# Interleaving the two groups of the SSD's B and C products on TensorE, over three pairs of banks

## The reference

```python
def ssd_chunked(x, a, bm, cm):
    ...
    scores = jnp.einsum('bclhn,bcshn->bhcls', cm, bm) * jnp.exp(segsum(a))
    y_diag = jnp.einsum('bclhs,bcshp->bclhp', scores, x)
    ...
def ssd_direction(xs, dt, a, bm, cm, reverse):
    heads_per_group = SSD_HEADS // SSD_GROUPS
    y = ssd_chunked(prep(xs * dt[..., None]), prep(dt * a),
                    prep(jnp.repeat(bm, heads_per_group, axis=2)),
                    prep(jnp.repeat(cm, heads_per_group, axis=2)))
```

## Time and profile before

| | |
|---|---|
| median of 3 runs | 2627.54 us (2627.06 to 2630.75) |
| span of the profiled execution, first to last instruction | 2628.6 us |
| TensorE busy | 2483.0 us, 94% |
| VectorE busy | 1365.9 us, 52% |
| ScalarE, GpSimd busy | 784.3 us, 1057.0 us |
| mean granted TensorE clock | 0.974 |
| CB stage, first load to end of last copy, layer 0 | 124.10 to 134.99 us |
| CB stage, layer 1 | 1431.64 to 1442.53 us |

### The profile page before, as it was taken

The page is one execution under the profiler, slowest core; times in us unless marked ns, Lnnn a source line. Parts: engine busy times, 40 slices in busy tenths (PEclk is TensorE's granted clock), DMA queues, the critical chain, the costliest instruction groups (busy, mean ns, idle before and its releaser), DMA issues.

```text
span 2628.6 us, 41897 instructions
## 1 busy us (share of the span) xinstructions
PE 2483.0 (94%) x17212; PEld 2196.8 (84%) x17212; DVE 1365.9 (52%) x2461; ACT 784.3 (30%) x1320; POOL 1057.0 (40%) x584
## 2 busy tenths in 40 slices
PE   7999989899999999999989999888999999999999
PEld 7866777677788899999988767776777888999999
DVE  8467755555544754441074677555554447444410
ACT  3233222244333222222222332222443332222221
POOL 4322333175653244444433223322756423444443
PEclk9999999999899999999999999999998999999999
DMA  4211100100000122233221111011000002222233
GB/s 147 65 41 37 45 33 25 57 1 1 25 25 17 57 89 89 90 95 97 97 73 57 41 41 43 31 33 49 1 1 26 24 17 65 89 89 90 96 96 106
DMA packets 40076, 144.39 MB, mean 55 GB/s; under 512 B 4432, under 2 KB 4560, under 8 KB 39760
## 3 DMA queue, kind: packets, MB, share of 16 engines
q1 hardware_dynamic: 39888, 141.72, 16.8%
HBM read 139.60 MB, written 2.10 MB: 54 GB/s over the span
## 4 chain that ended last, share of the span: by engine, by line
PE 80%; DVE 13%; issue 4%; ACT 2%; POOL 1%; DMA 1%; SPq 0%; DVEq 0%; ACTq 0%; POOLq 0%
PE pb L553 60%; PE pb L833 8%; DVE mbuf L1267 3%; PE pb L681 3%; PE pb L824 3%; PE pb L743 2%; DVE kh L1206 2%; PE pb L821 1%; DVE ebuf L1251 1%; PE pb L622 1%; PE pb L723 1%; DVE proj L1189 1%; DVE proj L1216 1%; POOL parts L439 1%; DVE mbuf L1272 1%
## 5 line engine op out<-in xcount | busy, mean ns | idle before, releaser
L439 POOL TENSOR_TENSOR parts<-raw,parts 128x1024 fp32r<-128x1024 f32 x248 | 607.3, 2449 | 1085.6 <-ACT parts L993 1085.2
L553 PE MATMUL pb<-mix,parts 128*128 128x264 f32 x5376 | 837.9, 295 | 29.2 <-POOL parts L439 18.9
L553 PE MATMUL pb<-proj_r,parts 128*128 128x264 f32 x6208 | 854.1, 285 | 1.0 <-POOL parts L439 1.0
L553 PEld LDWEIGHTS pb<-proj_r,parts 128*128 128x128 f32 x6208 | 798.3, 189 | 1.5 <-issue 1.4
L553 PEld LDWEIGHTS pb<-mix,parts 128*128 128x128 f32 x5376 | 728.6, 194 | 68.5 <-issue 43.4
L993 ACT ACTIVATE parts<-raw 128x1024 fp32r<-128x1024 f32 x248 | 262.4, 1058 | 822.1 <-PE pb L553 822.0
L833 PE MATMUL pb<-v_tok,mbuf 128*128 128x64 f32 (+3 forms) x1600 | 235.8, 284 | 3.4 <-DVE o_tok L1359 1.3
L833 PEld LDWEIGHTS pb<-v_tok,mbuf 128*128 128x128 f32 (+1 forms) x1600 | 203.9, 189 | 37.6 <-issue 15.8
L956 ACT ACTIVATE ebuf<-ebuf 128x528 f32<-128x528 f32 (+4 forms) x240 | 111.0, 464 | 336.7 <-DVE ebuf L1251 203.7
L974 ACT ACTIVATE ebuf<-pb,negmax 128x528 f32<-128x528 f32 x160 | 112.2, 701 | 330.2 <-DVE negmax L1331 330.2
L1194 DVE TENSOR_TENSOR h<-h,pb 128x528 f32<-128x528 f32 x48 | 33.7, 703 | 261.7 <-PE pb L553 261.7
(11 more groups left out here) (173 smaller groups left out, 2643.9 us busy)
## 6 DMA issues: line engine op xcount, KB each, us to landing
raw<-w_stream SPq DMA_DIRECT2D x250, 512.0 KB, 3.5
w_head<-w_heads SPq DMA_DIRECT2D x8, 512.0 KB, 5.0
h<-x_t SPq DMA_DIRECT2D x8, 264.0 KB, 6.5
out_t<-h SPq DMA_DIRECT2D x8, 256.0 KB, 4.8
con<-consts SPq DMA_DIRECT2D x1, 1652.5 KB, 10.1
par<-params SPq DMA_DIRECT2D x1, 340.0 KB, 4.5
con<-consts SPq DMA_DIRECT2D x1, 128.0 KB, 6.6
```

The costliest lines, as they stand in the source:

```text
L439: nc.gpsimd.tensor_tensor(parts[:, n % PARTS, 1, :], w, parts[:, n % PARTS, 0, :].bitcast(FP32), ALU.subtract).then_inc(split.sem, 1)
L553: last = nc.tensor.matmul(pb[rows_, 2 * p + a, 0:HALF], lhs_t, rhs[:, a * HALF:(a + 1) * HALF], start=start, stop=stop)
```

## The change

TensorE now issues the products by token tile. For each j it waits once, until 2j - 1 copies are done, and then issues four matmuls: the first half of the columns for group 0 and for group 1, then the second half for group 0 and for group 1. Product 2j + g goes to pair 1 + (2j + g) mod 3, so banks 2 to 7 are in use, and since bank 7 held the results for `cols`, there is a wait for `cols_ready`. The product's count (`cb_ps`) is raised by its second half. VectorE copies in the same new order. The numbers of matmuls, of copies and their shapes stay.

```diff
-                for g in range(SSD_G):
-                    r = slice(64 * g, 64 * g + 64)
-                    for j, (a, w) in enumerate(TILES):
-                        pe.wait_ge(tr_evac.sem, tr_evac.at(l, TR_X + NT))
-                        pe.wait_ge(cb_ready.sem, cb_ready.at(l, max(g * NT + j - 1, 0)))
-                        product(1 + (g * NT + j) % 2, tile_of(proj, BM, a, a + w, r), tile_of(proj, CM, rows_=r), True, True,
-                                slice(0, w)).then_inc(cb_ps.sem, 1)
+                pe.wait_ge(tr_evac.sem, tr_evac.at(l, TR_X + NT))
+                for j, (a, w) in enumerate(TILES):
+                    pe.wait_ge(cols_ready.sem, cols_ready.at(l, 1))
+                    pe.wait_ge(cb_ready.sem, cb_ready.at(l, max(2 * j - 1, 0)))
+                    for b in range(2):
+                        for g in range(SSD_G):
+                            r = slice(64 * g, 64 * g + 64)
+                            last = nc.tensor.matmul(pb[0:w, 2 + 2 * ((2 * j + g) % 3) + b, 0:HALF], tile_of(proj, BM, a, a + w, r),
+                                                    tile_of(proj, CM, b * HALF, (b + 1) * HALF, r), start=True, stop=True)
+                            if b == 1:
+                                last.then_inc(cb_ps.sem, 1)
...
-                for g in range(SSD_G):
-                    for j, (_, w) in enumerate(TILES):
-                        dve.wait_ge(cb_ps.sem, cb_ps.at(l, g * NT + j + 1))
-                        nc.vector.tensor_copy(halves(cb(g, j, 0, T, slice(0, w))), pair(1 + (g * NT + j) % 2, slice(0, w))).then_inc(cb_ready.sem, 1)
+                for j, (_, w) in enumerate(TILES):
+                    for g in range(SSD_G):
+                        dve.wait_ge(cb_ps.sem, cb_ps.at(l, j * SSD_G + g + 1))
+                        nc.vector.tensor_copy(halves(cb(g, j, 0, T, slice(0, w))), pair(1 + (2 * j + g) % 3, slice(0, w))).then_inc(cb_ready.sem, 1)
```

## The result

The change made the kernel slower: 2636.98 us (median of 5, 2633.21 to 2639.3) against 2629.07 (median of 5, 2627.06 to 2630.75). The ratio is 1.0029, with a 95% interval from 1.0016 to 1.0041, so 0.3%: 7.6 us by the ratio, 7.9 between the medians. That is small, but clear of the runs' noise. I had forecast 2627.4 with no measurable change, and a range up to 2633.8.

What follows compares the result with a forecast made beforehand. TensorE was taken to bound the kernel, the CB stage being paced by a TensorE-VectorE round trip. Base 2627.54 us minus 0.1 (side by side with half the load effect) gave 2627.4, range 2624.0 to 2633.8.

Steps and rivals of the forecast that it cites:

- Side by side: CB stage: the two groups' passes overlap on different array rows; -0.1 us with half the load effect, chance 0.56.
- round trip of 2.02 us: CB stage: load to copy 1.19, copy 0.71, wake 0.12 per two products; three pairs do not shorten it.
- in-turn case: CB stage: passes follow one another whatever their rows; period 2.46 us, +3.9 in all; chance 0.22 at full clock.
- load effect: CB stage, side by side: weight loads may become the limit, 0.11 us more per block, +0.44 over four blocks.
- lower bound: CB stage with groups side by side: period again 2.02 us, -0.27 per layer, -0.5 us in all.
- the other parts cost nothing: Around the CB stage: `cols_ready` long satisfied, GpSimd's L507 covered, no DMA moved, only short copies move on VectorE; no cost.
- 7 us of cover: Behind the CB stage: GpSimd's L507 and L509 finish some 7 us before the row broadcast, their first reader, loads.
- clock rival: CB stage: passes in turn and the clock falls there; +6.3 us in sum, 2633.8, chance 0.12.
- attention stage: Window 640 to 660, cited against a clock fall: clock stays 1.00 while 40 passes stream 8.8 of 20 us.
- price of 1.2 us per spell of 3.4 us: CB stage, passes in turn: 3.4 us at half clock do 0.90 blocks in place of 1.38, losing 1.2 us.
- faster rival: CB stage: VectorE copies run back to back and set the pace; -4.8 us in all, 2622.7, chance 0.04.
- My base: Whole kernel: the starting time added to, 2627.54 us, median of the three runs of the kernel before.

Runs made afterwards that it cites:

- e1: Changed kernel with both groups' products on partitions 0 to 63, so no neighbouring passes differ in rows; ratio to the kernel before 1.0032.
- e4: Changed kernel with GpSimd's two instructions behind the tenth product also waiting for the SSD loop's second weights; ratio to the kernel before 1.0010.
- e9: Changed kernel with GpSimd's first instruction behind the tenth product also waiting for the ninth copy; ratio to the kernel before 1.0006.
- e2: Changed kernel with two unread matmuls behind each of the first four blocks, where TensorE waits; ratio to the kernel before 1.0017.
- e3: Changed kernel's product order and three pairs, but each product whole and waiting for the copy three back; ratio to the kernel before 0.9996.
- e5: Kernel before with GpSimd's two instructions behind the tenth product also waiting for the SSD loop's second weights; ratio to the kernel before 1.0001.
- e7: Changed kernel with e2's unread matmuls and e4's GpSimd wait for the second weights; ratio to the kernel before 0.9988.
- e6: e3's whole products over three pairs plus e4's GpSimd wait for the second weights; ratio to the kernel before 0.9976.
- e8: e6 plus six unread matmuls behind the tenth product; 2621.19 us against 2632.26 for the kernel before, ratio 0.9958.
- e10: Kernel before with e4's GpSimd wait and six unread matmuls behind the tenth product (bank 6); ratio to the kernel before 0.9981.

## Why the prediction was wrong

- **The stage's mechanics were right.** Side by side was right (0.75 us for eight loads), so was the round trip of 2.02 us that three pairs don't shorten (2.02 measured), and the in-turn case (2.46 worked out, 2.47 in e1). The load effect that I added (0.11 per block) did not appear. At full clock the first three blocks of both layers ran as in the lower bound, and in layer 0 of e4, where the clock held to the end, the whole stage took 10.49 us, against 10.62 in that bound (the last two copies take 1.31 us together, where I had 1.42).
- **The step that failed most is "the other parts cost nothing".** I looked at GpSimd's L507 only for who reads its result, and found 7 us of cover. What mattered was whom GpSimd disturbs: after the edit the ninth and tenth products end nearly together, so the tenth product is ready while VectorE has the ninth copy still ahead, and GpSimd starts 1.21 us ahead of the end of the last copy, in place of 0.64. That is 0.57 us, and it changes who is first in the next two encounters. Cost, together with the longer low clock behind the stage: 3.8 and 3.5 us on the run-in. Moving GpSimd back in e9 took 2.9 and 3.8 of run-in away, and the ratio from 1.0029 to 1.0006. It was in no rival; the range had no term for it.
- **The clock rival was tied to the wrong condition.** I gave it only to passes in turn, with 0.12, and cleared the side-by-side case by the attention stage, where 40 passes fill 44% of the time at clock 1.00. But that window has TensorE busy for 19.90 of its 20 us: other matmuls run between. The clock fell in both cases. It seems to decide less than the hold: with the clock held in e2's stage the ratio went from 1.0029 to 1.0017. The price of 1.2 us per spell of 3.4 us was near the +1.23 of layer 0's stage by chance, since it was worked out for passes in turn, and the stage was at low clock for 5.8 us. The whole spell lasted 17 us in place of 3.4. The hold probably lengthens it, since it keeps TensorE waiting right behind the stage: with GpSimd moved in e9 the spells were 10.2 us. But e1 had 17 and 13.7 us without a hold of the first two weights, so this is argued and not shown. The parts can't be summed exactly: e2 and e9 take back 0.12% and 0.23% of the 0.29% and overlap within their intervals.
- **The faster rival was priced too high.** VectorE as the bound came true in e3, at 8.02 us (8.5 worked out), once each product waited for the copy three back. The block-wise wait of this change keeps it out of reach.
- **The chances** gave 0.16 to slower. The mechanism that I had for it, a fall of the clock in the stage, was a real one, but its condition was false and it was not the main one. My base, the median of three runs, was also 1.5 us below the median of five; that alone would not have brought the result into the range.

What stays open: how much of the 7.6 us is hold and how much is clock, beyond the estimate above; why the clock in e5 falls 11.3 us behind the first load, 2 us sooner than in the kernel before; and what decides over the single spells of low clock elsewhere in the kernel, which set e4's total above before, and e7's below it, against their measured stretches.

On the hold, the Trainium skill, SBUF — State Buffer, section "Who interferes with whom", says that a VectorE instruction with two SBUF inputs contends with a GpSimd instruction that reads SBUF, over a shared read interface that is locked exclusively, and that the order of issue decides who blocks. The traces agree: 1.55 and 2.65 us for VectorE when GpSimd was first, 1.67 in place of 1.30 for GpSimd when it was second.

## What to carry to other kernels

When an edit makes an engine finish earlier or two results come together, list every instruction that this releases on VectorE and GpSimd, and look who will be first at their next meeting; a shift of half a microsecond, with the low clock behind it, cost 3 to 4 us per layer here. More bank pairs help only if the wait is moved back as well: waiting per product for the copy three back gave a stage of 8.0 us where waiting per block gave 10.5 at full clock (e4, layer 0). And where TensorE must wait for some microseconds, unread matmuls into a free bank can keep the clock up: six of them took 1.3 us off each run-in (e6 to e8), and 2.2 in the order of the kernel before (e5 to e10).

## What the runs showed of the hardware

- Float32 matmuls on different halves of the array's rows run side by side even though each has two passes: eight 64-row loads in 0.75 us against 1.63 us on the same rows, with the first copy 1.20 against 1.64 us behind the first load.
- The granted clock fell from 1.00 to 0.50 behind the stage's first load by 6.3 and 8.1 us in the changed kernel (loads at rest for 1.24 of each 2.02 us), by 8.3 and 6.4 in e9 and 8.5 in e4's layer 1 with the same blocks, and by 5.8 and 7.9 in e1 (0.83 of 2.47). In e4's layer 0, again with the same blocks, it held until the stage was over, so these times are what was seen and not a rule. In the stage of the kernel before (0.39 of 2.02) it held in both layers, in e5 too.
- A VectorE instruction with two operands in SBUF that starts just behind a GpSimd `TENSOR_TENSOR` ends a time behind it that grows with its own columns: 0.16 us for 144 (kernel before), 0.30 for 272 (e9), 0.43 for 400 and 0.56 for 528 (changed kernel). GpSimd's first instruction (L507, 1.53 us) holds for less than its recorded length: started 1.35 us into it, the first weights before took their 0.76; started 0.15 us into it, the third weights of e8 took 0.77 for 0.50.
- A pair of copies, the second of which finds its source ready, takes 1.32 us where each takes 0.71 alone; eight in a row take 5.23, 0.65 each (e3).
